# Front stage of a two-layer hybrid block: x normalised token-major before the transposes, convolution and gate fed straight from PSUM

## The chip, the cores and the metric

One core of a Trainium2 chip runs the kernel. The metric is the device time of one execution in microseconds (us), here as the median of three runs. TensorE (PE) multiplies, VectorE (DVE) and ScalarE (ACT) work element by element, GpSimd (POOL) does small side work, and SyncE's queue (SP) issues the loads and stores. TensorE writes to PSUM (banks of 128 partitions by 512 fp32 values), which VectorE and ScalarE can read; everything else lives in SBUF.

## The reference, cut to what matters

A block of two layers over 512 tokens of width 1024. The change touches the first mixer only, in layer 0:

```python
def rmsnorm(x, w):
    xf = x.astype(jnp.float32)
    xf = xf * lax.rsqrt(jnp.mean(xf * xf, axis=-1, keepdims=True) + NORM_EPS)
    return (xf * w.astype(jnp.float32)).astype(x.dtype)
...
def ssd_mixer(u, w_in, conv_w, conv_b, dt_bias, a_log, d_skip, norm_w, w_out):
    proj = u @ w_in
    z = proj[..., :SSD_D_INNER]
    xbc = jax.nn.silu(dwconv_centred(proj[..., SSD_D_INNER:SSD_D_INNER + SSD_CONV_DIM], conv_w, conv_b))
    dt_raw = proj[..., SSD_D_INNER + SSD_CONV_DIM:].astype(jnp.float32)
    ...
    y = y.reshape(bsz, seq, SSD_D_INNER) * jax.nn.silu(z.astype(jnp.float32))
...
    for i in range(DEPTH):
        u = rmsnorm(h, mix_norm_w[i])
        ...
        h = h + mix
        h = h + conv_ffn(rmsnorm(h, ffn_norm_w[i]), ...)
        h = h + per_layer_embed(h, p[i], ...)
    return rmsnorm(h, final_norm_w)
```

The convolution runs over the tokens, channel by channel, with 5 taps centred on the token. The mixer (a chunked scan in both directions) has 4 groups of 8 heads.

## The kernel before, in words

Everything is kept transposed: channels on the partitions, the 512 tokens along the free dimension. `h[:, m, :]` (m = 0..7) is the residual. Each projection is computed in fp32 quality from three fp32r products: the weights are split into `w_hi` (ACT, line 974, `hi(u)`) and `w_lo` (DVE, line 1315, `lo(u)`), the input into `uh` and `ul`, and `product` (PE, lines 1916 to 1918) issues w_hi·uh, w_hi·ul and w_lo·uh.

The work of PE is cut into *units*: one load of up to 128x1024 weights, which feeds 24 matmuls of 128x512. A *pair* is two units (the two halves of the contraction) that fill two PSUM tiles. Units are numbered in one sequence (`Plan.unit`), and `w_raw`, `w_hi`, `w_lo` have two buffers each: `hi(u)` waits until unit u-2 has been multiplied, `lo(u)` waits for `hi(u)`, the load of u waits for `lo(u-2)`. `hi_to` and `lo_to` issue them at fixed places of ACT's and DVE's programs.

All projections go through `ring`, four PSUM banks in rotation: tile t is written into bank t % 4, and PE waits on the semaphore `evac` until tile t-4 has been taken out. `evac` counts the tiles in their order. The other PSUM banks are `pe_e` (2), `pe_y` and `pe_s`.

**Start.** SP loads x (one 2 MB DMA), then 19 small DMAs of parameters into `stage` and `step_in`, 3 more small ones, then the weights. PE waits for all 19, transposes the seven parameter tiles, then x, tile by tile, into `ring`. For each of the 8 tiles DVE copies it to `h`, ACT squares it and makes `uh`, DVE makes `ul`, POOL adds up the squares; PE sums them over the partitions with a ones matrix (`pe_s`), DVE and ACT turn that into `rstd`, the same row of 512 values on every partition (`rstd_of(0)`). Unit 0 is the `dt` projection (64 columns). `uh` and `ul` carry x times the norm's weight but not `rstd`: every projection of this layer is multiplied by `rstd` as it is taken out of PSUM.

**Each group g** has 3 pairs `xbc` (x in two pairs, B and C in the third), 2 pairs `z` and, from g = 1, the four `out` units of the group before. For an `xbc` pair DVE multiplies both tiles by `rstd` into `cin` (line 1430, this frees the banks), ACT does the first tap (line 1056), DVE the other four on each tile (line 1440, 8 instructions), ACT the silu (line 1065). For a `z` pair DVE multiplies by `rstd` into `zs` (`take_z`, line 1452) and ACT applies silu in place. After the third pair come transposes of x and B, the products with the masks, the states and their decays, and for each of 4 head pairs the decay rows (ACT, lines 1087 and 1097), their weighting (DVE, 1486 to 1488) and the output products (PE, 2059); at the end of the group DVE and ACT normalise y (lines 1592 to 1604), while PE works on the first units of the next group.

After the four groups come two feed-forward blocks, the gates and the second mixer. The change does not touch their arithmetic.

## Time and profile before

| | |
|---|---|
| time, median of 3 runs | 1782.2 us (1780.02 to 1782.22) |
| span of the profiled execution | 1782.5 us |
| busy in it | PE 87%, weight loads 70%, DVE 71%, ACT 44%, POOL 13% |
| first matmul of unit 0 (`dt`) / of the first `xbc` unit | 47.29 / 56.51 us |
| first `xbc` pair taken out of PSUM from | 69.35 us |
| first `z` pair of group 0 taken from | 102.00 us |
| end of group 0, 1, 2 (line 1592) | 190.91, 320.55, 449.98 us |

The profiled execution has no other time beside its span, and the span lies 0.3 us above the median, inside the spread of the runs. Times in the rows below count from the first instruction. The table is read as a sequence: the start until 56.51 us, then group 0, then three groups of about 130 us each, then 1200 us of other work.

### The profile page before, as it was taken

How to read it: one execution, taken by the hardware profiler on the slowest of the kernel's cores; microseconds unless marked ns; L12 is line 12 of the kernel's file. 1: busy time of each engine (PE TensorE's matmuls, PEld its weight loads, DVE VectorE, ACT ScalarE, POOL GpSimd, SP SyncE). 2: the span in 40 equal slices, each digit the busy share in tenths (PEclk: the TensorE clock that was granted, in tenths of full speed). 3: DMA queues.
4: the chain of work that ended last, by engine and by line, in shares of the span. 5: the costliest groups of instructions: out<-in, count | busy, mean ns of one | idle time of the engine just before them, and what ended most of it. 6: DMA issues, size and time to landing. Idle time of an engine off the chain costs nothing.

```text
span 1782.5 us, 20153 instructions
## 1 busy us (share of the span) xinstructions
PE 1551.1 (87%) x7275; PEld 1248.1 (70%) x7275; DVE 1257.2 (71%) x1479; ACT 784.4 (44%) x1339; POOL 225.0 (13%) x224
## 2 busy tenths in 40 slices
PE   3875886987986889999998776889999999999996
PEld 1663765755754668878886564879787888888875
DVE  4577767767866788887888687897467666664355
ACT  3348456456465445522444424231235555543242
POOL 1144000000000480002007311000010000001000
PEclk7897998998998899999998988795999999999998
DMA  2223313313312343353343565693322333233231
GB/s 73 83 67 128 100 63 115 92 54 118 95 48 71 77 101 95 117 183 124 120 156 131 189 219 189 186 277 84 92 97 83 100 100 94 94 100 101 89 95 65
DMA packets 192169, 198.99 MB, mean 112 GB/s; under 512 B 47822, under 2 KB 178462, under 8 KB 187998
## 3 DMA queue, kind: packets, MB, share of 16 engines
q1 hardware_dynamic: 192094, 198.01, 35.9%
q8 instruction: 45, 0.74, 0.2%
q14 instruction: 30, 0.25, 0.0%
HBM read 169.47 MB, written 28.51 MB: 111 GB/s over the span
## 4 chain that ended last, share of the span: by engine, by line
PE 66%; DVE 15%; ACT 9%; DMA 5%; issue 3%; SPq 1%; DVEq 0%; ACTq 0%
PE ring L1916 19%; PE ring L1917 19%; PE ring L1918 19%; ACT rows L1087 3%; DVE w_lo L1315 3%; ACT rows L1097 3%; PE pe_s L2161 2%; PE ring L2145 2%; DMA w_raw<-in_ple_w_gate 2%; DMA rows<-log_decays 1%; ACT w_hi L974 1%; PE pe_s L2155 1%; PE pe_y L2059 1%; DVE cc L1440 1%; DVE cc L1806 1%
## 5 line engine op out<-in xcount | busy, mean ns | idle before, releaser
L974 ACT ACTIVATE w_hi<-w_raw 128x1024 fp32r<-128x1024 f32 (+1 forms) x233 | 239.6, 1028 | 621.7 <-PE ring L1918 572.4
L1916 PE MATMUL ring<-uh,w_hi 128*128 128x512 f32 (+1 forms) x1160 | 462.0, 398 | 41.4 <-DVE w_lo L1315 30.0
L1917 PE MATMUL ring<-ul,w_hi 128*128 128x512 f32 (+1 forms) x1160 | 455.6, 393 | 0.0
L1918 PE MATMUL ring<-uh,w_lo 128*128 128x512 f32 (+1 forms) x1160 | 454.9, 392 | 0.0
L1315 DVE TENSOR_TENSOR w_lo<-w_raw,w_hi 128x1024 fp32r<-128x1024 f32 (+1 forms) x233 | 281.7, 1211 | 180.2 <-ACT w_hi L974 179.9
L1916 PEld LDWEIGHTS ring<-uh,w_hi 128*128 128x128 f32 (+1 forms) x1160 | 219.8, 190 | 99.5 <-DVE w_lo L1315 27.5
L1918 PEld LDWEIGHTS ring<-uh,w_lo 128*128 128x128 f32 (+1 forms) x1160 | 219.7, 189 | 47.5 <-issue 0.6
L1917 PEld LDWEIGHTS ring<-ul,w_hi 128*128 128x128 f32 (+1 forms) x1160 | 220.0, 190 | 47.1 <-issue 2.1
L1916 PE MATMUL ring<-gh,w_hi 128*128 128x512 f32 x480 | 189.5, 395 | 19.3 <-DVE w_lo L1315 17.6
L1918 PE MATMUL ring<-gh,w_lo 128*128 128x512 f32 x480 | 188.0, 392 | 0.0
L1917 PE MATMUL ring<-gl,w_hi 128*128 128x512 f32 x480 | 188.0, 392 | 0.0
L1806 DVE SCALAR_TENSOR_TENSOR cc<-cin,par,cc 128x512 f32<-128x512 f32 x176 | 128.3, 790 | 1.0 <-ACT cc L1251 1.0
L1916 PEld LDWEIGHTS ring<-gh,w_hi 128*128 128x128 f32 x480 | 91.0, 190 | 41.7 <-DVE w_lo L1315 18.9
L1795 DVE TENSOR_TENSOR cin<-ring,rstd 128x512 f32<-128x512 f32 x88 | 56.7, 686 | 77.3 <-PE ring L1918 77.3
L1918 PEld LDWEIGHTS ring<-gh,w_lo 128*128 128x128 f32 x480 | 90.8, 189 | 19.4
L1917 PEld LDWEIGHTS ring<-gl,w_hi 128*128 128x128 f32 x480 | 91.1, 190 | 18.5
L1087 ACT ACTIVATE rows<-rows,ad_seq 128x128 f32<-128x128 f32 x256 | 76.4, 386 | 19.0 <-DMA rows<-log_decays 19.0
L2059 PE MATMUL pe_y<-rows,xseq 128*64 128x128 f32 x256 | 38.3, 372 | 52.3 <-DVE xT L1500 50.1
L1097 ACT ACTIVATE rows<-rows,dt_seq 128x128 f32<-128x128 f32 x256 | 76.4, 386 | 0.0
L1251 ACT ACTIVATE cc<-cin,par 128x512 f32<-128x512 f32 x88 | 66.7, 806 | 16.1 <-DVE cin L1795 16.1
L2059 PEld LDWEIGHTS pe_y<-rows,xseq 128*64 128x64 f32 x256 | 32.8, 191 | 56.5 <-DVE xT L1500 53.0
L753 POOL TENSOR_TENSOR var<-sq 128x512 f32<-128x512 f32 x7 | 10.0, 1425 | 484.1 <-ACT sq L990 423.0
(280 smaller groups left out, 2157.8 us busy)
## 6 DMA issues: line engine op xcount, KB each, us to landing
w_raw<-in_ffn_w_up SPq DMA_DIRECT2D x88, 512.0 KB, 3.5
w_raw<-in_ffn_w_down SPq DMA_DIRECT2D x40, 512.0 KB, 3.5
w_raw<-in_ssd_w_in SPq DMA_DIRECT2D x32, 512.0 KB, 4.0
rows<-log_decays SPq DMA_DIRECT2D x16, 1024.0 KB, 6.0
s_tables<-tab SPq DMA_DIRECT2D x16, 1024.0 KB, 5.3
slot<-s_tables SPq DMA_DIRECT2D x16, 1024.0 KB, 7.4
w_raw<-in_ssd_w_out SPq DMA_DIRECT2D x16, 512.0 KB, 3.5
w_raw<-in_ple_w_gate SPq DMA_DIRECT2D x16, 512.0 KB, 3.5
```

Source lines behind the costliest of these rows:

```text
L974: act.activation(w_hi[u % 2][:, 0:n], w_raw[:, u % 2, 0:n], ACT.Copy).then_inc(hi_done, 1)
L1087: act.activation(row, row, ACT.Relu, scale=-1.0, bias=cs_seq[:, c, at:at + 1]).then_inc(fall_done, 1)
L1097: act.activation(row, row, ACT.Exp, scale=-1.0, bias=dt_ln[:, c, at:at + 1]).then_inc(exp_done, 1)
L1251: act.activation(cc[:, 2 * half + j, :], cin[:, j, 1:1 + SEQ], ACT.Identity, scale=dcol(i * 2 + (C_FCW + c)), bias=dcol(i * 2 + (C_FCB + 2 ...
L1315: dve.tensor_tensor(w_lo[u % 2][:, 0:n], w_raw[:, u % 2, 0:n], w_hi[u % 2][:, 0:n].bitcast(F32), ALU.subtract).then_inc(lo_done, 1)
L1795: dve.tensor_tensor(cin[:, j, 2:2 + SEQ], bank(t + 2 * half + j), rstd[:], ALU.mult).then_inc(evac, 1)
L1806: dve.scalar_tensor_tensor(out=cc[:, 2 * half + j, :], in0=cin[:, j, 1 + tap:1 + tap + SEQ], scalar=dcol(i * 2 + (C_FCW + c)), in1=cc[:, 2 ...
L1916: pe.matmul(o, wh[:, k, c], rh[:, k0 + k, :], start=first and k == 0, stop=False)
L1917: pe.matmul(o, wh[:, k, c], rl[:, k0 + k, :], start=False, stop=False)
L1918: mm_ = pe.matmul(o, wl[:, k, c], rh[:, k0 + k, :], start=False, stop=last and k == nk - 1)
L2059: mm_ = pe.matmul(pe_y[64 * k:64 * k + 64, c * P:(c + 1) * P], xseq[:, c, (2 * hp + k) * HD:(2 * hp + k + 1) * HD], rows_[n % 3][:, 0, k, ...
L2145: mm_ = pe.matmul(ring[:, 2 * (b % 2) + a, NCH * g:NCH * g + NCH], slots[b % 4][:, 0, at:at + P], ul[:, b % 3, g, :], start=True, stop=True)
```

## The change

Part one, the start. x is loaded in four DMAs of 128 tokens, ahead of 9 parameter DMAs; the other 10 and the 3 small ones go behind the first two loads of weights. While tokens are still on the partitions, DVE squares and sums each piece (`tensor_tensor_reduce`), one tiny chain gives 1/rms of every token, and DVE scales x by it into `xn`. PE transposes `xn` into `ring`; ACT makes `uh` and DVE `ul` directly from PSUM, so `uh`/`ul` now hold the normalised input and no later projection needs `rstd`. The raw x, which the residual `h` needs, is transposed apart: half of it at once into the four PSUM banks that are free then (`spare`), half after the first pair, with the remaining parameter tiles; ACT copies these out. The `dt` unit moves behind the third `xbc` pair.

Part two, in every group. The centre tap (shift 0) is done by ACT from PSUM, and the other four taps by DVE from PSUM, on the part of the row where they fall inside the sequence; `evac` now counts at the last tap of a tile. `z` is read by ACT's silu straight from PSUM. `cin` and `take_z` with their 24 and 16 multiplications fall away.

Some semaphores of the second layer are shared where before there was one each; SP now waits for three saves (`t_late`) where it waited for two.

```diff
-        tile("params", 2)
+        tile("params", 1)
         tile("x", 8)
-        tile("dt", 1, True)
         for g in range(groups):
             tile(("xbc", g), 6, True)
+            if g == 0:
+                tile("dt", 1, True)
...
-            sp.dma_start(x_in[:], A["x"][0].rearrange("(b p) d -> p b d", p=P)).then_inc(in_x, 16)
+            for b in range(SB):
+                sp.dma_start(x_in[:, b, :], A["x"][0, b * P:b * P + P, :]).then_inc(in_x[b], 16)
...
-                    xbc_loads(0, 0, 6)
+                    xbc_loads(0, 0, 2)
+                    late_params()
+                    xbc_loads(0, 2, 6)
+                    load(U["dt"], rows(w_in, 0, KD, XBC0 + CONV_T * P, 2 * HEADS), k=KD)
...
+            act.wait_ge(x_step, X_VAR)
+            act.activation(x_ss[:], x_ss[:], ACT.Sqrt).then_inc(x_std, 1)
             for m in range(KD):
-                squares(0, m)
-                u_hi(0, m, uh0)
-            std(0)
+                if m == 4:
+                    hi_to(1)
+                act.wait_ge(filled, FILL["x"] + m + 1)
+                if m == 0:
+                    act.wait_ge(evac, 1)
+                act.activation(uh0[:, m, :], bank(T["x"] + m), ACT.Identity, scale=col(C_MIX + m)).then_inc(x_uh, 1)
...
+            def spares(n0, n1):
+                for n in range(n0, n1):
+                    act.wait_ge(spare_full, n + 1)
+                    dst = h[:, n, :] if n < KD else (par[:, 2 * P:6 * P], par[:, 6 * P:7 * P])[n - KD]
+                    act.activation(dst, spare(n)[:, 0:dst.shape[1]], ACT.Copy).then_inc(spare_taken, 1)
+            spares(0, 4)
...
                     hi_to(u + 2 * i + 3)
                     if g == 0:
                         if i == 0:
+                            spares(4, KD + 2)
+                            act.wait_ge(spare_taken, KD + 2)
                             vec(V_STEP, par[:, C_STEP:C_STEP + S5G], ACT.Exp)
...
-                        act.wait_ge(evac, T[("xbc", g)] + 2 * i + j + 1)
+                        act.wait_ge(unit_done, u + 2 * i + 2)
...
-                        act.activation(cc[:, q % 4, :], cin[:, q % 2, 0:SEQ], ACT.Identity,
-                                       scale=col(C_CONVW + chans[j]), bias=col(C_CONVB + chans[j])).then_inc(tap0, 1)
+                        act.activation(cc[:, q % 4, :], bank(T[("xbc", g)] + 2 * i + j), ACT.Identity,
+                                       scale=col(C_CONVW + 2 * CONV_T + chans[j]), bias=col(C_CONVB + chans[j])
+                                       ).then_inc(tap0, 1)
...
+                    act.wait_ge(unit_done, z + 2 * i + 2)
+                    if g:
+                        act.wait_ge(yl_done, GT * g)
+                    act.wait_ge(evac, T[("z", g, i)])
                     for j in range(2):
-                        act.wait_ge(evac, T[("z", g, i)] + j + 1)
-                        act.activation(zs[:, 2 * i + j, :], zs[:, 2 * i + j, :], ACT.Silu).then_inc(z_silu, 1)
+                        act.activation(zs[:, 2 * i + j, :], bank(T[("z", g, i)] + j), ACT.Silu).then_inc(evac, 1)
...
+            for b in range(SB):
+                dve.wait_ge(in_x[b], 16)
+                dve.tensor_tensor_reduce(out=xn[:, b, :], in0=x_in[:, b, :], in1=x_in[:, b, :], scale=1.0, scalar=0.0,
+                                         op0=ALU.mult, op1=ALU.add, accum_out=x_ss[:, b:b + 1]).then_inc(x_step, 1)
...
-                    for j in range(2):
-                        dve.tensor_tensor(cin[:, j, 2:2 + SEQ], bank(T[("xbc", g)] + 2 * i + j), rstd[:], ALU.mult
-                                          ).then_inc(evac, 1)
                     lo_to(u + 2 * i + 3)
-                    for tap in range(1, 5):
+                    for n, shift in enumerate(SHIFTS):
...
+                            op = dve.scalar_tensor_tensor(
+                                out=cc[:, q % 4, a:b], in0=bank(T[("xbc", g)] + 2 * i + j)[:, a + shift:b + shift],
+                                scalar=col(C_CONVW + (2 + shift) * CONV_T + chans[j]), in1=cc[:, q % 4, a:b],
+                                op0=ALU.mult, op1=ALU.add)
+                            op.then_inc(*((taps, 1) if n < 3 else (evac, 1)))
```

VectorE at the start of the program, before the change, up to the first `lo`. The names in it are the tiles above; x8 is a count of equal neighbours.

```order
L1353 COPY stage<-step_in 64x128
L1345 COPY par<-ring 128x512
L1357 COPY par<-ring 128x384
L1345 COPY h<-ring 128x512
L1329 SCALAR_TENSOR_TENSOR ul<-h,par,uh 128x512
L1345 COPY h<-ring 128x512
L1329 SCALAR_TENSOR_TENSOR ul<-h,par,uh 128x512
```

VectorE at the same place after the change; the ISA rows are the sums of squares and the reading of their sums (four of each).

```order
L1391 ISA xn,x_ss<-x_in 128x1024
L1391 ISA x_ss 128x1
L1394 TENSOR_SCALAR x_ss<-x_ss 128x4
L1382 COPY par<-ring 128x256
L1397 RECIPROCAL x_rs<-x_ss 128x4
L1400 TENSOR_SCALAR xn<-x_in,x_rs 128x1024 x4
L1407 SCALAR_TENSOR_TENSOR ul<-ring,par,uh 128x512 x4
L1352 TENSOR_TENSOR w_lo<-w_raw,w_hi 128x1024
L1407 SCALAR_TENSOR_TENSOR ul<-ring,par,uh 128x512 x4
```

The eight copies to `h` have left VectorE, the squares are sums over whole rows, and the first `lo` stands after the fourth `ul`.

VectorE where group 0 ends and group 1 begins, before the change: the normalisation of y, then the first pair's convolution.

```order
L1315 TENSOR_TENSOR w_lo<-w_raw,w_hi 128x1024
L1600 SCALAR_TENSOR_TENSOR zs<-xT,par,ytmp 128x512 x4
L1604 TENSOR_TENSOR yl<-zs,yh 128x512 x4
L1430 TENSOR_TENSOR cin<-ring,rstd 128x512 x2
L1315 TENSOR_TENSOR w_lo<-w_raw,w_hi 128x1024
L1440 SCALAR_TENSOR_TENSOR cc<-cin,par,cc 128x512 x8
L1315 TENSOR_TENSOR w_lo<-w_raw,w_hi 128x1024
L1430 TENSOR_TENSOR cin<-ring,rstd 128x512 x2
```

The same place after the change.

```order
L1352 TENSOR_TENSOR w_lo<-w_raw,w_hi 128x1024
L1632 SCALAR_TENSOR_TENSOR zs<-xT,par,ytmp 128x512 x4
L1636 TENSOR_TENSOR yl<-zs,yh 128x512 x4
L1352 TENSOR_TENSOR w_lo<-w_raw,w_hi 128x1024
L1481 SCALAR_TENSOR_TENSOR cc<-ring,par,cc 128x510 x2
L1481 SCALAR_TENSOR_TENSOR cc<-ring,par,cc 128x511 x4
L1481 SCALAR_TENSOR_TENSOR cc<-ring,par,cc 128x510 x2
L1352 TENSOR_TENSOR w_lo<-w_raw,w_hi 128x1024 x2
```

The two `cin` rows are gone; nothing else has changed its place there.

ScalarE in group 0 between its first two rounds of `hi` and the second pair, after the change (before it, the two L1061 and L1087 rows followed the `hi` rows directly).

```order
L988 ACTIVATE w_hi<-w_raw 128x1024 x2
L1029 ACTIVATE h<-pe_e 128x512 x2
L1029 ACTIVATE h<-pe_y 128x512
L1029 ACTIVATE h<-pe_s 128x512
L1029 ACTIVATE par<-pe_e 128x512
L1029 ACTIVATE par<-pe_e 128x128
L1061 ACT_TABLE_LOAD
L1061 ACTIVATE v<-par 128x64
L1087 ACTIVATE cc<-ring,par 128x512 x2
```

Six copies out of the spare banks now stand ahead of the first pair's centre taps.

## Rows read from the trace of the kernel before

**Rows 1.** Busy time by stretch: engine busy (count), granted clock, DMA share.

```profile
core 0: us, PE busy (x) PEld busy (x) DVE busy (x) ACT busy (x) POOL busy (x), PEclk, DMA share, GB/s
0.00:47.26 47.26, 14.14 (x45) 8.27 (x46) 21.26 (x26) 14.60 (x21) 8.69 (x20) 0.71 0.21 69
47.26:54.64 7.38, 7.31 (x24) 3.88 (x24) 0.00 (x0) 0.00 (x0) 0.00 (x0) 0.76 0.23 71
54.64:56.51 1.87, 0.00 (x0) 0.00 (x1) 1.87 (x3) 1.06 (x1) 0.00 (x0) 1.00 0.00 0
56.51:69.35 12.84, 12.84 (x49) 10.44 (x50) 2.31 (x2) 1.06 (x1) 0.00 (x0) 0.87 0.41 122
69.35:101.97 32.62, 32.62 (x146) 26.96 (x145) 27.55 (x36) 20.36 (x26) 15.08 (x25) 1.00 0.31 83
...
190.90:320.55 129.65, 107.86 (x473) 81.44 (x472) 94.40 (x122) 71.26 (x170) 2.53 (x2) 0.93 0.29 90
```

**Rows 2.** Timeline of the start: start, length, engine, line, what; idle before it.

```profile
0.81 0.45 SPq L451 DMA_DIRECT2D x_in<-in_x  x1
10.36 0.60 SPq L475 DMA_DIRECT2D step_in<-in_s_log_step  x1
14.66 3.32 PE L1944 MATMUL ring<-eye,x_in 128*128 128x128 f32 x20
20.52 1.12 PE L1944 MATMUL ring<-eye,x_in 128*128 128x128 f32 x4 [2.55 <-DVE h L1345]
24.93 1.25 DVE L1329 SCALAR_TENSOR_TENSOR ul<-h,par,uh 128x512 fp32r<-128x512 f32 x1 [1.31 <-ACT uh L994]
```

**Rows 3.** DMA issues of the start: count, size, median us from issue to landing.

```profile
x_in<-in_x SPq DMA_DIRECT2D x1, 2048.0 KB, 8.0
w_raw<-in_ssd_w_in SPq DMA_DIRECT2D x4, 512.0 KB, 5.2
```

**Rows 4.** Stretches behind the pause at 54.64 us, columns as in Rows 1.

```profile
59.00:61.00 2.00, 2.00 (x6) 1.52 (x6) 0.00 (x0) 0.00 (x0) 0.00 (x0) 0.50 0.99 321
61.00:63.00 2.00, 2.00 (x10) 1.65 (x9) 0.00 (x0) 0.00 (x0) 0.00 (x0) 1.00 0.18 61
```

**Rows 5.** Groups by form, 0 to 620 us: count, busy, mean ns, idle before.

```profile
L1493 DVE SCALAR_TENSOR_TENSOR xT<-xT,d_col,pe_e 128x512 f32<-128x512 f32 x16 | 11.8, 740 | 0.0
L1600 DVE SCALAR_TENSOR_TENSOR zs<-xT,par,ytmp 128x512 f32<-128x512 f32 x16 | 10.9, 745 | 0.0
L1392 DVE TENSOR_SCALAR rows<-rows,hvec 64x512 f32<-64x512 f32 x1 | 0.5, 478 | 0.0
L1022 ACT ACTIVATE rows<-pe_e 64x512 f32<-64x512 f32 x1 | 0.6, 590 | 5.1 <-PE pe_e L1969 5.1
L1031 ACT ACT_TABLE_LOAD x2 | 2.6, 1283 | 0.0
```

**Rows 6.** Timeline at the start of group 1, VectorE and then TensorE.

```profile
201.88 1.28 DVE L1430 TENSOR_TENSOR cin<-ring,rstd 128x512 f32<-128x512 f32 x2
203.08 1.21 DVE L1315 TENSOR_TENSOR w_lo<-w_raw,w_hi 128x1024 fp32r<-128x1024 f32 x1
204.22 5.38 DVE L1440 SCALAR_TENSOR_TENSOR cc<-cin,par,cc 128x512 f32<-128x512 f32 x8
209.52 1.21 DVE L1315 TENSOR_TENSOR w_lo<-w_raw,w_hi 128x1024 fp32r<-128x1024 f32 x1
...
204.35 0.50 PE L1916 MATMUL ring<-uh,w_hi 128*128 128x512 f32 x1 [1.65 <-DVE w_lo L1315]
...
210.79 0.50 PE L1916 MATMUL ring<-uh,w_hi 128*128 128x512 f32 x1 [0.70 <-DVE w_lo L1315]
```

**Rows 7.** Timeline behind the second z pair of group 1, VectorE, then ScalarE.

```profile
249.04 1.29 DVE L1452 TENSOR_TENSOR zs<-ring,rstd 128x512 f32<-128x512 f32 x2 [8.34 <-PE ring L1918]
250.25 2.35 DVE L1315 TENSOR_TENSOR w_lo<-w_raw,w_hi 128x1024 fp32r<-128x1024 f32 x2
252.51 0.68 DVE L1345 COPY car<-ring 128x512 f32<-128x512 f32 x1
...
263.36 1.06 ACT L974 ACTIVATE w_hi<-w_raw 128x1024 fp32r<-128x1024 f32 x1 [1.38 <-PE ring L1918]
```

More of the change, by code:

```diff
@@ L74, in __init__ @@
         units = 0
-        mixer = [("dt", 1)]
+        mixer = []
         for g in range(groups):
-            mixer += [(("xbc", g), 6), (("z", g), 4)] + ([(("out", g - 1), 4)] if g else [])
+            mixer += [(("xbc", g), 6)] + ([("dt", 1)] if g == 0 else [])
+            mixer += [(("z", g), 4)] + ([(("out", g - 1), 4)] if g else [])
         mixer += [(("out", groups - 1), 4)]
@@ L170, in bidir_hybrid_kernel @@
         step_in = sb("step_in", [S5G, 2], where=start)
+        x_ss = sb("x_ss", [P, SB], where=start)
+        x_rs = sb("x_rs", [P, SB], where=start)
+        xn = sb("xn", [P, SB, D], where=start)
         start.close()
@@ L423, in unit_size, with saved_u @@
             return 1024
+        def saved_u(b):
+            return (u_saved[b % 3], 16 * (b // 3) + 16) if b < 6 else (u_saved[b - 3], 16)
         def loads_by(u):
@@ L601, in s5_loads @@
                     sp.wait_ge(tab_saved[i], 16 * NB)
-                for n in range(NB):
+                for n in range(5):
                     sp.wait_ge(t_saved[n], 16)
@@ L1063, in _ @@
                         dst = xT[:, 2 * i + j, :] if i < 2 else (bT, cT)[j][:]
-                        act.wait_ge(taps, 8 * (3 * g + i) + 6 + j + 1)
+                        act.wait_ge(evac, T[("xbc", g)] + 2 * i + j + 1)
                         act.activation(dst, cc[:, q % 4, :], ACT.Silu).then_inc(silu, 1)
+                if g == 0:
+                    dt_take()
                 hi_to(z + 3)
@@ L1425, in _ @@
                     chans = [g * GT + 2 * i, g * GT + 2 * i + 1] if i < 2 else [INNER // P + g, INNER // P + GROUPS + g]
[L1426 to L1431 removed]
                     lo_to(u + 2 * i + 3)
[L1433 removed]
+                    for n, shift in enumerate(SHIFTS):
                         for j in range(2):
                             q = 6 * g + 2 * i + j
[L1436 removed]
+                            if n == 0:
                                 dve.wait_ge(tap0, q + 1)
                             else:
[L1439 to L1453 removed]
+                                dve.wait_ge(taps, 6 * pr + 2 * (n - 1) + j + 1)
+                            a, b = max(0, -shift), SEQ - max(0, shift)
+                            op = dve.scalar_tensor_tensor(
[3 more added lines that the diff above has]
+                            op.then_inc(*((taps, 1) if n < 3 else (evac, 1)))
+                    lo_to(u + 2 * i + 4)
                 def take_out(g, i):
@@ L1538, in _ @@
                 if g:
-                    take_z(1)
                     lo_to(z + 5)
+                    dve.wait_ge(evac, T[("state", g, 0)])
                 for n in range(6):
@@ L1995, in _ @@
                     for kg in range(2):
+                        if g == 0 and i == 0:
+                            pe.wait_ge(evac, T["x"] + 4 * kg + 4)
                         product(u + 2 * i + kg, T[("xbc", g)] + 2 * i, 4, 4 * kg, uh0, ul0, first=kg == 0, last=kg == 1)
+                        if g == 0 and (i, kg) == (0, 1):
+                            late_transposes()
                         if g and (i, kg) == (0, 0):
                             group_square(g - 1, GT - 1)
+                if g == 0:
+                    product(U["dt"], T["dt"], KD, 0, uh0, ul0, tiles=1, width=2 * HEADS)
                 z_product(0)
```

217 lines of the change are left out of this document (110 added, 107 removed).

## The prediction, written before the changed kernel ran

> **What bounds the kernel now.** I read the busy times by stretch first [rows 1]. Before 56.51 us PE is busy for 21.5 us, and in two thirds of that with things that are not projections: the start is a chain, not a throughput problem. From 69.35 to 101.97 us PE is full: three pairs, 144 matmuls of 512 columns in 32.62 us, so 0.2265 us each, 5.44 us a unit and 10.87 us a pair. In a later group PE works 107.9 of 129.65 us and DVE 94.4, so each group has stretches in which something else ends the wait. To find which, I read the timeline.
>
> At the start [rows 2, 3] x lands 8.0 us after its issue, at 8.8 us, but PE stands still until the last of 19 parameter DMAs, issued at 10.36 us, has been spread; then the x tiles crawl because a tile passes PE, DVE, ACT and DVE in turn, and `ul` takes 1.25 us. At the start of group 1 [rows 6] PE waits for DVE: `yl` ends at 201.88, then come `cin` (1.20 us to the next row), `lo`, eight taps (5.30 us), `lo`, and only then, at 210.79, PE starts the fifth unit of the group (0.70 us idle on the row, and 1.65 us at the unit before). From there PE runs without a gap to the z pair. Behind the second z pair [rows 7] PE and ACT wait for DVE again: 1.21 us of `zs`, two `lo` in 2.26 us, then the first state copy at 252.51; everything down to ACT's `hi` at 263.36, which waits for PE, hangs on it.
>
> **The start, step by step.** The first xbc pair comes out at 69.35 us now. After the change:
>
> - x has landed at 8.8 us as before, since the four DMAs move the same 2 MB ahead of all else. The last piece's sum of squares: no row shows this instruction. Bounds: 1.21 us (two SBUF inputs, 1024 long, the `lo` of [rows 6]) and twice that. I take 1.2, it has the same inputs: 10.0.
> - Three tiny operations over DVE and ACT and the copy of two parameter tiles; 0.2 us each and 0.4 us by estimate from the lengths in [rows 5]: 11.1. ACT's table for the square root is loaded ahead, while it waits.
> - Four scalings of 128x1024: one SBUF input and a column scalar took 0.478 us for 512 [rows 5]. Bounds 0.75 and 1.21 each. I take 0.75, the same form: 14.1.
> - First four tiles. PE's transposes run at 0.166 us each at the full clock and about 0.23 at the lower [rows 2], so 0.66 to 0.93 a tile. With the lower one, 17.8; then `uh` 0.7 (an estimate: a bit over the 0.59 of ACT's row in [rows 5]), `hi` 1.05, `lo` 1.2 [rows 6, 7]: unit 0 starts near 20.8. The first weights land 5.2 us after an issue at about 7 [rows 3], so they wait, not PE. The other four tiles need about 4.5 us on ACT and DVE and are hidden behind unit 0.
> - Units 0 and 1: 10.9 us, plus a start at the lower clock. In this trace the granted clock was 0.50 in a stretch behind a pause of 1.87 us [rows 1, 4], and the first pair took 12.84 us in place of 10.88 (its two units less the boundary). I add 1.9.
>
> The pair ends at 33.6 us: 35.7 us earlier.
>
> **What is given back in group 0.** Behind the first pair PE has work that it had done before: 21 transposes (3.6 us at 0.166; 4.8 at 0.23), and the `dt` unit, 24 matmuls of 512 columns, now in the middle of a full PE: 5.4 us. The transposes ask for little, so I expect the clock to drop once more behind them as at 54.64 to 56.51: 1.6 us. ACT stands longer: after `hi` six copies (0.55 to 0.59 each [rows 5], together with `hi` 4.3 us), a table load and the exponential (1.5), then the taps. With 0 at the end of the first pair: centre taps 5.8 to 7.3, DVE's eight taps 6.6 to 12.0 and `lo` to 13.2. PE is at 14.5 by then (3.6 of transposes and a pair), so ACT's queue is covered by 1.3 us; if the cover went, the price would be that excess. The third pair is finished at 25.4, `dt` at 30.8. Its taps are the ones that count: two of the four banks are held until the last tap, and z's first unit must wait for one of them. `hi` of the unit ahead to 26.5, two small sines, centre tap, then taps from 27.7, the first tile's last at 32.5: 1.7 us of waiting. Sum given back: 3.6 + 5.4 + 1.6 + 1.7 = 12.3. Net gain before the end of z's first pair: 35.7 - 12.3 = 23.4 us. The rest of group 0 runs as before: there z's silu waits for a table load (1.28), which takes the place of the two multiplications.
>
> **What each later group gains.** At its start `cin` goes, 1.2 us of DVE in a chain that PE waits for [rows 6]. The centre tap on ACT no longer waits for `cin`, and is ready before `lo` ends. The banks: PE's fifth unit writes where the first pair stood, and now needs its last tap, at 203.0 + 5.3 = 208.3; the `lo` behind it ends at 209.5 anyway, so the hold costs nothing, by 1.2 us of cover. For the next two pairs DVE needs 5.3 + 2.3 us in PE's 10.9, and ACT's `hi`, silu, `hi`, centre tap about 4; taps start near 7 and 2 us after the pair, and end 3 us before their bank is asked for. Behind the second z pair `take_z` goes and one `lo` moves ahead of the wait: the copy that stood 3.47 us behind the pair stands behind `hi` and `lo`, 1.06 + 1.2: 1.2 us. ACT's two silus there stay where they were, behind one `hi`, so the decays behind them start no later, and at 263.36 ACT had been idle for 1.38 us, so it lets the gain through. Sum 2.4 us for each of groups 1, 2, 3: 7.2 us. What a tap costs from PSUM is the one price this rests on. In [rows 5] the same instruction with a PSUM input took 740 ns, without one 745: no difference.
>
> The Trainium skill gives VectorE a longer fixed time for PSUM sources, 120 cycles against 58 (VectorE: DVE Perf Modes, the section on the TRN2 errata). That speaks against this change: by it the eight taps are an estimated 0.5 us longer, the gain of three groups is 5.7 us, and the total is 1753. By the rows there is nothing to subtract; they decide.
>
> In the second layer SP waits for a third save, a few us of an interval in which it is ahead; I count nothing. Sum: 23.4 + 7.2 = 30.6 us off 1782.5, which has the median's place within 0.3: **1751.6**.
>
> **Rivals.**
>
> *The groups give nothing* (0.15): the hold of banks, or ACT's reordered queue, eats the 2.4 us. For it: PE's cover at the fifth unit is 1.2 us. Against: DVE's chain is shorter by whole instructions. Time 1782.5 - 23.4 = 1759.
>
> *The sums of squares run at half rate* (0.12): each of the four takes 2.4 us. Pieces land some 1.5 us apart, so the last one ends near 13.4 in place of 10.0, and the whole start moves by 3.4: 1755. For it: an instruction that adds up beside two SBUF inputs has no row. Against: none either. The Trainium skill says that this family with two non-bf16 SBUF sources halves its throughput (Vector Engine (DVE) Microarchitecture Reference, Points that are easy to get wrong); no trace here shows it.
>
> *The clock stays up and the banks are free in time* (0.10): 1.9 + 1.6 + 1.7 us fewer, 1746. For it: after the first 51 us PE has few pauses. Against: the row of 0.50 came after one below 2 us.
>
> *Slower: taps from PSUM run as `ul` did beside POOL, 1.25 us each* (0.03). Then each pair needs 8 x 1.25 + 2.3 us of DVE, more than PE's 10.9, and with ACT's 3.5 us in series a pair of banks comes free 2.6 us late, 12 times (31 us), and the chain into the fifth unit is 4.7 us longer, 4 times (19 us): 1752 + 50 = 1802. It decides from about 1.05 us a tap. Against it: the 740 ns row, taken while PE ran.
>
> *The start doesn't shorten* (0.01): the four pieces of x would have to land as late as everything together did. Against: 8.0 us for 2 MB. Time 1775 to 1785.
>
> **How the numbers follow.** Forecast as worked out: 0.59. Low end: the clock rival and one more us in each group, 1743. High end: half-rate squares together with the scalings at 1.21 (1.9 us), or no group gain with a little of either: 1762. Beyond that lie some of the mixed cases and the slower one. Faster by over 0.2% (3.6 us, about what a measurement of this kernel can tell from no change): 0.96; the same 0.01; slower 0.03.
>
> **What would show each step.** The first xbc matmul near 21 us, and the end of the first pair near 34; an idle PE of 1 to 2 us ahead of z in group 0 that ends with a tap; z's first pair of group 0 finished near 78.5. The fifth unit of group 1 starts 7.7 us after `yl` ends (8.9 now); the first state copy 2.3 us behind z's second pair; group lengths (from one line-1624 instruction to the next) of 127.2 us. Taps of 0.74 us. Wrong it would be if taps take over 1 us, if PE waits for banks between xbc pairs, or if x lands in pieces later than 9 us.

## The result, and the profile after

The changed kernel takes 1754.6 us (median of 4 runs, 1748.3 to 1756.3) against 1782.2 us before: ratio 0.983, 95% interval 0.981 to 0.986. The forecast was 1751.6 us, range 1743 to 1762, faster at 0.96. Sign and time came out as predicted, the time with some luck: single terms of the start were off by 1.0 to 1.6 us both ways and partly cancelled, the groups gave less than their 7.2 us in this trace, and runs of one kernel differ by as much as single terms (the next four runs of the changed kernel had a median of 1749.0 us).

The profiled execution took 1753.23 us with a span of 1751.4 us, 31.1 us less than the 1782.5 us before; between the medians of the runs it is 27.6 us. The windows by stretch (core 0; us, then busy time of each engine with its count, granted clock, DMA share, GB/s) answer to [rows 1]:

```profile
0.00:22.29 22.29, 12.48 (x51) 9.43 (x51) 15.88 (x27) 8.31 (x12) 2.40 (x15) 1.00 0.51 162
22.29:34.89 12.60, 12.60 (x48) 10.16 (x49) 3.65 (x5) 3.15 (x6) 0.00 (x0) 0.86 0.38 114
34.89:37.58 2.69, 2.65 (x23) 2.44 (x22) 1.23 (x1) 2.43 (x5) 0.00 (x0) 1.00 0.09 27
37.58:77.70 40.12, 38.48 (x170) 30.13 (x170) 22.52 (x30) 21.49 (x31) 8.79 (x25) 1.00 0.31 84
166.55:295.67 129.12, 110.00 (x473) 82.78 (x472) 88.35 (x111) 70.88 (x170) 2.53 (x2) 0.93 0.28 90
295.67:422.55 126.88, 107.94 (x473) 81.36 (x472) 88.35 (x111) 70.83 (x170) 2.53 (x2) 0.93 0.29 92
```

The first `xbc` pair ends at 34.9 us, not 69.35. Behind it stand 2.7 us of transposes at the full clock. A later group has 88.4 us of DVE in place of 94.4, the 6 us of the removed multiplications, but lasts 129.1 or 126.9 us, in place of 129.65.

The timeline of the start (start, length, engine, line, what, idle time before it and its releaser), against [rows 2]:

```profile
4.57 1.23 DVE L1391 CUSTOM_DVE_ANT_0 xn<-x_in 128x1024 f32<-128x1024 f32 x1 [1.59 <-DMA x_in<-in_x]
8.50 1.23 DVE L1391 CUSTOM_DVE_ANT_0 xn<-x_in 128x1024 f32<-128x1024 f32 x1
...
11.13 0.42 DVE L1382 COPY par<-ring 128x256 f32<-128x256 f32 x1 [1.19 <-PE ring L1973]
11.68 2.74 DVE L1400 TENSOR_SCALAR xn<-x_in,x_rs 128x1024 f32<-128x1024 f32 x4
...
15.79 3.23 DVE L1407 SCALAR_TENSOR_TENSOR ul<-ring,par,uh 128x512 fp32r<-128x512 f32 x4 [1.37 <-ACT uh L1022]
19.20 1.23 DVE L1352 TENSOR_TENSOR w_lo<-w_raw,w_hi 128x1024 fp32r<-128x1024 f32 x1 [0.19 <-ACT w_hi L988]
20.73 2.73 DVE L1407 SCALAR_TENSOR_TENSOR ul<-ring,par,uh 128x512 fp32r<-128x512 f32 x4 [0.30 <-ACT uh L1022]
22.29 0.47 PE L1948 MATMUL ring<-uh,w_hi 128*128 128x512 f32 x1 [1.89 <-DVE ul L1407]
```

The sum of squares of a piece (the custom instruction) takes 1.23 us for 1024 columns, so the half-rate rival is out. The last line is the surprise of the start: `lo` of unit 0 is done at 20.4 us (the forecast had 20.8), and PE still waits for `ul`, its first product starting at 22.29 behind 1.89 us of idleness.

TensorE's one wait in group 0 ahead of z, then VectorE and TensorE at the start of group 1 against [rows 6], and VectorE's state copy behind the second z pair against [rows 7]:

```profile
66.55 0.47 PE L1948 MATMUL ring<-uh,w_hi 128*128 128x512 f32 x1 [1.64 <-DVE cc L1481]
...
177.53 1.22 DVE L1352 TENSOR_TENSOR w_lo<-w_raw,w_hi 128x1024 fp32r<-128x1024 f32 x1
178.67 5.34 DVE L1481 SCALAR_TENSOR_TENSOR cc<-ring,par,cc 128x510 f32<-128x510 f32 x8
183.92 1.21 DVE L1352 TENSOR_TENSOR w_lo<-w_raw,w_hi 128x1024 fp32r<-128x1024 f32 x1
...
178.80 0.50 PE L1948 MATMUL ring<-uh,w_hi 128*128 128x512 f32 x1 [0.44 <-DVE w_lo L1352]
185.19 0.50 PE L1948 MATMUL ring<-uh,w_hi 128*128 128x512 f32 x1 [0.61 <-DVE w_lo L1352]
...
225.65 0.68 DVE L1382 COPY car<-ring 128x512 f32<-128x512 f32 x1
```

`yl` ends at 177.53 and the fifth unit starts at 185.19: 7.7 us, the forecast to the tenth (8.9 before). Eight taps from PSUM take 5.34 us, from SBUF they took 5.38 (with 510 or 511 columns each now, 512 then).

### The profile page after: what moved, and what is told of

It is laid out like the page before. It is cut to its first block, busy times and chain, and to the rows that moved or that the text cites. A ratio compares the mean times of both kernels' runs of the same rounds, so it can differ in the third digit from the quotient of the medians.

```text
span 1751.4 us, 20143 instructions
## 1 busy us (share of the span) xinstructions
PE 1551.1 (89%) x7301; PEld 1248.7 (71%) x7301; DVE 1227.2 (70%) x1441; ACT 780.9 (45%) x1340; POOL 213.7 (12%) x219
## 4 chain that ended last, share of the span: by engine, by line
PE 69%; DVE 13%; ACT 9%; DMA 5%; issue 3%; SPq 0%; DVEq 0%; ACTq 0%
PE ring L1948 20%; PE ring L1949 20%; PE ring L1950 20%; ACT rows L1124 3%; ACT rows L1134 2%; PE pe_s L2216 2%; DVE w_lo L1352 2%; PE ring L2200 2%; DMA w_raw<-in_ple_w_gate 2%; ACT w_hi L988 1%; DMA rows<-log_decays 1%; DVE cc L1481 1%; PE pe_y L2114 1%; PE pe_s L2210 1%; DVE ytmp L1626 1%
## 5 line engine op out<-in xcount | busy, mean ns | idle before, releaser
L1948 PE MATMUL ring<-uh,w_hi 128*128 128x512 f32 x1160 | 461.3, 398 | 32.6 <-DVE w_lo L1352 23.2
L1949 PE MATMUL ring<-ul,w_hi 128*128 128x512 f32 x1160 | 455.0, 392 | 0.0
L1950 PE MATMUL ring<-uh,w_lo 128*128 128x512 f32 x1160 | 454.1, 391 | 0.0
L1948 PEld LDWEIGHTS ring<-uh,w_hi 128*128 128x128 f32 x1160 | 219.4, 189 | 88.6 <-DVE w_lo L1352 21.3
L1950 PEld LDWEIGHTS ring<-uh,w_lo 128*128 128x128 f32 x1160 | 219.4, 189 | 47.3
L1949 PEld LDWEIGHTS ring<-ul,w_hi 128*128 128x128 f32 x1160 | 219.6, 189 | 46.9 <-issue 1.7
L1288 ACT ACTIVATE cc<-cin,par 128x512 f32<-128x512 f32 x88 | 66.7, 805 | 12.7 <-DVE cin L1827 12.7
L1481 DVE SCALAR_TENSOR_TENSOR cc<-ring,par,cc 128x510 f32<-128x510 f32 (+1 forms) x96 | 64.1, 739 | 4.6 <-ACT cc L1087 4.6
```

The lines of the kernel that those rows point to most:

```text
L1288: act.activation(cc[:, 2 * half + j, :], cin[:, j, 1:1 + SEQ], ACT.Identity, scale=dcol(i * 2 + (C_FCW + c)), bias=dcol(i * 2 + (C_FCB + 2 ...
L1481: op = dve.scalar_tensor_tensor(out=cc[:, q % 4, a:b], in0=bank(T[("xbc", g)] + 2 * i + j)[:, a + shift:b + shift], scalar=col(C_CONVW + ( ...
L1948: pe.matmul(o, wh[:, k, c], rh[:, k0 + k, :], start=first and k == 0, stop=False)
L1949: pe.matmul(o, wh[:, k, c], rl[:, k0 + k, :], start=False, stop=False)
L1950: mm_ = pe.matmul(o, wl[:, k, c], rh[:, k0 + k, :], start=False, stop=last and k == nk - 1)
```

## Where the 31.1 us are

I follow marks that both traces have: VectorE's first `xseq` copy (the end of group 0's projections), the first addition of an output tile to `h` in each group (h0), the second (h1), and the group's end (the `var` instruction). All times in us, each a start from the timelines:

| mark | before | after | after, second trace (E1) |
|---|---|---|---|
| first product | 47.29 | 22.29 | 22.10 |
| first `xseq` copy | 104.34 | 80.02 | 78.26 |
| end of group 0 | 190.91 | 166.55 | 166.01 |
| end of group 3 | 575.47 | 546.43 | 544.56 |
| span | 1782.5 | 1751.4 | 1745.9 |

In the first trace 24.3 us are gained before group 0's `xseq`, 4.7 in groups 1 to 3, and 2.1 in the 1200 us behind group 3, where the change does nothing (1207.0 against 1205.0; 1201.3 in the second trace). So the start has its predicted 23.4 and 0.9 more, the groups have 4.7 of the predicted 7.2, and 2.1 are not the change's. That left two questions: what the groups' missing 2.5 us are, and which step of the start was misjudged.

## The experiments

**E1, the changed kernel again** (a_again). No edit.

> The changed kernel once more, for a second trace of it. In the first trace group 1 kept 24.9 us of the 27.0 us that it was ahead at the first output tile, because the granted clock was 0.82 to 0.87 in two stretches of 5 us near 230 and 250 us; group 2 had no such loss behind its output tile. If those stretches belong to the program, they stand at the same places again and the group ends lie within 0.2 us of 166.6, 295.7, 422.6 and 546.4. If the clock's drops depend on where a chip happens to be in its own rhythm, the work between them has the same durations, but group 1, 2 or 3 differ by 1 to 2 us from the first trace, and the total lies anywhere from 1748 to 1757.

1749.0 us (1747.6 to 1754.9, 4 runs). The group lengths changed places: 126.9, 129.1, 122.6, where the first trace had 129.1, 126.9, 123.9. In detail, h0 minus the end of the group before (A), h1 minus h0 (B), end of group minus h1 (C), groups 1, 2, 3:

| | A | B | C |
|---|---|---|---|
| before | 72.39, 72.39, 70.82 | 16.85, 16.85, 18.52 | 40.40, 40.19, 36.15 |
| after | 69.78, 69.94, 69.78 | 18.45, 16.84, 18.43 | 40.89, 40.10, 35.67 |
| after, E1 | 70.00, 69.83, 69.96 | 16.85, 18.47, 16.87 | 40.05, 40.75, 35.77 |

B has two values, 16.85 and 18.45, for the same instructions. The windows of group 1 around the same idle stretch (2.52 us in the first trace, 2.53 in the second) show why, the changed kernel's first trace first, then E1's:

```profile
223.33:226.99 3.66, 1.71 (x5) 0.40 (x4) 2.48 (x4) 3.57 (x9) 0.00 (x0) 1.00 0.03 7
226.99:231.33 4.34, 4.33 (x7) 2.13 (x8) 4.27 (x8) 4.32 (x12) 0.00 (x0) 0.61 0.36 115
240.33:247.01 6.68, 3.76 (x9) 1.15 (x8) 6.44 (x11) 6.68 (x25) 0.00 (x0) 1.00 0.00 0
247.01:252.33 5.32, 5.32 (x19) 4.28 (x20) 4.09 (x4) 5.32 (x20) 0.00 (x0) 0.68 0.01 3
```

```profile
223.01:226.68 3.67, 1.72 (x5) 0.55 (x4) 2.65 (x4) 3.67 (x10) 0.00 (x0) 1.00 0.07 20
226.68:231.22 4.54, 4.47 (x9) 2.28 (x10) 4.47 (x8) 4.51 (x13) 0.00 (x0) 0.65 0.29 99
240.01:246.69 6.68, 3.77 (x8) 1.15 (x7) 6.44 (x11) 6.68 (x25) 0.00 (x0) 1.00 0.00 0
246.69:252.01 5.32, 5.31 (x26) 4.47 (x27) 4.10 (x4) 5.32 (x20) 0.00 (x0) 1.00 0.01 3
```

Same work, same 6.68 us with 3.8 us of PE, but then 5.3 us with a mean clock of 0.68 in one and 1.00 in the other, and 1.6 us between them at h1. At the end of the group it is 2.2 us (129.12 against 126.90), since C differs too. The fall behind the states, in A, stood in all six groups of the two traces; the one in B comes and goes, as the theory of a rhythm has it, and the total fell in its 1748 to 1757. What decides it is not shown.

The start varies in the same way. In E1 the first `xbc` pair ran at the full clock:

```profile
22.10:33.12 11.02, 11.02 (x49) 9.05 (x50) 3.66 (x5) 3.15 (x6) 0.00 (x0) 1.00 0.44 130
```

It took 11.02 us there and 12.60 in the first trace, at a mean clock of 0.86.

**E2 and E3, the copies put back in groups 1 to 3** (b1, b2). E2 copies the convolution's banks to `cin` first (edit below, with the waits that belong to it); E3 also puts DVE's copies of the z banks back.

```diff
+                    if g:
+                        dve.wait_ge(unit_done, u + 2 * i + 2)
+                        dve.wait_ge(taps, t0)
+                        for j in range(2):
+                            dve.tensor_copy(cin[:, j, 2:2 + SEQ], bank(T[("xbc", g)] + 2 * i + j)).then_inc(evac, 1)
```

> As the changed kernel, but in groups 1 to 3 DVE first copies each convolution bank to SBUF and the taps read the copy. My theory (the copy stood on the path into the fifth unit of a group): the fifth unit starts 8.7 us after yl ends, in place of 7.5, and the first output tile of groups 1 to 3 comes 1.2 us later each time; total 3.6 us over the changed kernel, 1757. Rival, that the hold of banks costs as much as the copy: total unchanged at 1753, and PE waits before the z pair now in the changed kernel. Rival, that taps are dearer from PSUM: eight taps here take less than 5.30 us.

> As b1, and in groups 1 to 3 DVE copies the gate's banks before silu too, so that only the start and group 0 of the change are left. Theory: start and group 0 alone are worth 24 us and the groups 2.4 us each where no clock drop eats it; total 1760, 7 us over the changed kernel, the first state copy of group 1 stands 3.5 us behind the z pair, and the first output tile of group 1 is 24.4 us earlier than before the change, against 27.0 in the changed kernel. Rival, the clock gives the groups' gain back anyway: total 1755 to 1756, with group lengths within 0.5 us of the changed kernel's in sum.

E2: 1755.7 us (1753.2 to 1760.6), E3: 1759.9 us (1758.6 to 1760.3). E2's timeline at the start of group 1, VectorE then TensorE:

```profile
178.72 1.28 DVE L1479 COPY cin<-ring 128x512 f32<-128x512 f32 x2
179.92 1.22 DVE L1354 TENSOR_TENSOR w_lo<-w_raw,w_hi 128x1024 fp32r<-128x1024 f32 x1
181.05 5.39 DVE L1491 SCALAR_TENSOR_TENSOR cc<-cin,par,cc 128x512 f32<-128x512 f32 x8
...
181.19 0.50 PE L1964 MATMUL ring<-uh,w_hi 128*128 128x512 f32 x1 [1.63 <-DVE w_lo L1354]
187.63 0.50 PE L1964 MATMUL ring<-uh,w_hi 128*128 128x512 f32 x1 [0.70 <-DVE w_lo L1354]
```

The fifth unit starts 8.9 us behind `yl` (ending 178.72), and A is 70.97, 70.89, 70.91: 1.1 us more than the changed kernel, three times. That is the convolution's term (1.2 predicted). Both rivals of E2 fall by these marks; its total, 1.1 us over the changed kernel's first four runs and 6.7 over the next four, can't tell. In E3 the first state copy stands 61.6 us behind the end of group 0 (227.50 - 165.88), 1.2 more than E2's 60.4 (228.17 - 167.75), which is the gate's term; but its A is 73.41, 70.79, 70.79. The windows around the states of E3 in groups 1, 2 and 3 say what happened (TensorE only):

```profile
228.00:236.00 8.00, 7.16 (x15) 0.57 0.36 122
355.00:364.00 9.00, 5.79 (x19) 1.00 0.36 117
484.00:493.00 9.00, 5.79 (x18) 1.00 0.40 119
```

In groups 2 and 3 the clock did not fall there. The same holds for group 3 of the kernel before (70.82, clock 1.00 from 511 to 519 us) and for group 1 of E8 (68.33, clock 1.00 from 222 to 231 us). So A must be compared like for like: with a fall 72.39 against 69.8, without one 70.82 against 68.33. Both say 2.5 to 2.6 us at h0 for the two passes that the change took away, where the forecast had 2.4. (Group 1 of E3, 73.41, had the clock at a mean of 0.57 over 8 us and compares with none.) The lengths of whole groups with a fall in A and none in B say about the same: 129.64 and 129.43 us before, 126.88 and 126.90 after, 2.7 us less. The total of E3 came out at the theory's 1760; over the changed kernel's first median it is 5.3 us, and the lengths of its three groups are 4.9 us longer in sum, where the rival had them within 0.5.

**E4, x in one load.**

```diff
-            for b in range(SB):
-                sp.dma_start(x_in[:, b, :], A["x"][0, b * P:b * P + P, :]).then_inc(in_x[b], 16)
+            sp.dma_start(x_in[:], A["x"][0].rearrange("(b p) d -> p b d", p=P)).then_inc(in_x[0], 16)
```

> x comes in one DMA of 2 MB in place of four pieces, all else as in the changed kernel. Theory: the pieces let three of four sums of squares run under the load; with one load they start near 8.8 us and end at 13.9 in place of 9.7, PE's first product moves by 4.1 us, from 22.3 to 26.4, and the total is 1757. Rival, the first product waits for something else (weights, parameters, a bank): it moves by less than 2 us.

1760.0 us (1751.9 to 1767.5). E4's timeline:

```profile
8.74 1.23 DVE L1390 CUSTOM_DVE_ANT_0 xn<-x_in 128x1024 f32<-128x1024 f32 x1 [5.76 <-DMA x_in<-in_x]
...
13.53 0.42 DVE L1381 COPY par<-ring 128x256 f32<-128x256 f32 x1
14.11 2.74 DVE L1399 TENSOR_SCALAR xn<-x_in,x_rs 128x1024 f32<-128x1024 f32 x4
...
24.73 0.47 PE L1947 MATMUL ring<-uh,w_hi 128*128 128x512 f32 x1 [2.56 <-DVE ul L1406]
```

The sums end 3.7 us later (13.41 against 9.73), but the parameter copy no longer waits for PE, which costs 1.19 us in the changed kernel, and the first product moves by 2.4 us only. Loading in pieces is worth 2.4 us here because something else is next in line: neither the theory's 4.1 nor the rival's under 2. At the first `xseq` copy it is 2.6 us (80.86 against E1's 78.26, neither with a fall at the start). The total moved by more, within a wide spread (below).

**E5, E6 and E7, dearer taps** (taps_090, taps_130, taps_125). A write that nothing reads behind each tap, to test the price of the slower rival.

```diff
                             op.then_inc(*((taps, 1) if n < 3 else (evac, 1)))
+                            if 8 * pr + 2 * n + j:
+                                dve.wait_ge(padded, 8 * pr + 2 * n + j)
+                            dve.memset(cin[:, 0, 2:2 + 512], 0.0).then_inc(padded, 1)
```

> As the changed kernel, with a write of 128 columns (which nothing reads) behind every tap on DVE, so that a tap costs some 0.9 us in place of 0.67. My working puts the point from which banks are late at 1.05 us a tap: below it only the chain into the fifth unit grows, by 8 x 0.23 = 1.8 us in each of four groups, total 1753 + 7 = 1760, and PE has no new wait between convolution pairs. Rival, there is no cover and every tap's cost counts: 96 x 0.23 = 22 us, 1775.

> As taps_090, with a write of 512 columns, so that a tap costs some 1.3 us, as in the prediction's slower rival. That rival's price: banks come free late in every pair and the chain into the fifth unit is some 5 us longer; 1802, a little more at 1.3 than at 1.25 (1808), slower than the kernel before the change. If PE's own work still covers the hold between pairs, only the chain counts: 4 x 5 = 20 us, 1773, and PE waits for taps only ahead of the fifth unit.

> As taps_130 with a longer write behind each tap. That kernel's tap came every 1.09 us, not 1.3; this one should come near 1.25 us, the price of the prediction's slower rival. By its working: chain into the fifth unit 4 x 4.6 us, and banks late by 2.6 us, 12 times: 1754 + 50 = 1804. What the trace of the 1.09 us kernel suggests instead: PE waited for the chain into the fifth unit alone (4.10 us against 0.61) and for no bank between the pairs behind it, so 4 x 4.6 us plus what DVE's own 8 x 1.25 + 2.3 = 12.3 us a pair exceed PE's 10.9, 1.4 us for the second and third pair of each group: 1754 + 18 + 11 = 1783.

The three kernels' taps came every 0.69, 1.09 and 1.30 us, not 0.9, 1.3 and 1.25: a write of 128 columns added 0.03 us to the tap's period of 0.66, where I had reckoned with 0.23. So the first (1757.2 us, 2 runs) tests nothing; its A of 69.95 to 70.24 is the changed kernel's. At 1.09 us the time is 1775.4 us (1768.4 to 1782.6), near the 1773 of the reading in which only the chain into the fifth unit counts; at 1.30 us it is 1792.4 us (1786.0 to 1794.2), slower than before the change (ratio 1.005, 1.002 to 1.007). TensorE in group 1 of the last:

```profile
201.59 0.79 PE L1954 MATMUL ring<-uh,w_hi 128*128 128x512 f32 x1 [5.85 <-DVE w_lo L1353]
214.78 0.50 PE L1954 MATMUL ring<-uh,w_hi 128*128 128x512 f32 x1 [0.24 <-DVE w_lo L1353]
227.45 1.09 PE L2067 MATMUL ring<-eye,xT 128*128 128x128 f32 x8 [1.49 <-ACT cT L1098]
```

PE waits for the chain into the fifth unit (5.85 us, 0.61 in the changed kernel) and hardly for a bank: in groups 1 to 3 `cc` releases none of its waits of this stretch; in group 0 it does, 4.86 us at 74.81. The rival's 50 us at 1.25 had too much in the banks; at a still dearer 1.30 it is 38. The second working of E7's expectation, redone afterwards for 1.30 (4 x 5.0 us of chain, 8 pairs with 12.7 us of DVE in PE's 10.9), gives 1754.6 + 20 + 14 = 1789. Between the two measurements a straight line crosses 1782.2 at 1.17 us a tap.

**E8 and E9, the start reordered** (weights_early, weights_params). E8 puts ACT's `hi_to(0)` and DVE's `lo_to(0)` ahead of the x tiles (edit below), E9 also moves DVE's copy of the first parameters behind the first scaling.

```diff
             act.activation(x_ss[:], x_ss[:], ACT.Sqrt).then_inc(x_std, 1)
+            hi_to(0)
             for m in range(KD):
-                if m == 4:
+                if m == 6:
                     hi_to(1)
...
             dve.wait_ge(evac, 1)
+            lo_to(0)
             for m in range(KD):
-                if m == 4:
-                    lo_to(0)
```

> As the changed kernel, but ACT rounds the first weights and DVE takes the rest of them before the x tiles, where both wait for PE. In the changed kernel the first product started at 22.29 us, when the sixth x tile was taken: its output bank is that tile's. Theory: the 1.23 us that DVE spent on the weights between the fourth and fifth tile were on that path, and it starts at 20.9; the first pair ends 1.4 us earlier, total 1.4 us less (1752). Rival, the product waits for the weights' landing: the x tiles are late instead and the product starts at 22.3 or later.

> As weights_early, and DVE copies the first two parameter tiles behind the first scaling of x instead of ahead of the reciprocal, where it had waited 1.19 us for PE. Theory: the scalings end 0.9 us earlier and so does the first product: 20.0 us, total 2.3 us below the changed kernel (1751). Rival, PE's transposes for the parameters are late and hold the x tiles in any case: no difference to weights_early.

E8's timeline:

```profile
14.03 1.22 DVE L1353 TENSOR_TENSOR w_lo<-w_raw,w_hi 128x1024 fp32r<-128x1024 f32 x1
15.40 5.02 DVE L1407 SCALAR_TENSOR_TENSOR ul<-ring,par,uh 128x512 fp32r<-128x512 f32 x6 [0.15 <-ACT uh L1023]
...
20.57 0.47 PE L1948 MATMUL ring<-uh,w_hi 128*128 128x512 f32 x1 [0.70 <-DVE ul L1407]
```

The first product starts at 20.57 us, 1.5 to 1.7 us earlier, when the sixth `ul` is done: the wait at 22.29 was one for the output bank, and the theory holds.

E8 also shows what a fall behind the states is worth. Its group 1 had none, and its group 2 had one: A is 68.33 and 69.92, but B is 18.02 and 16.87, and the groups last 126.88 and 126.84 us. In group 1 VectorE, asked earlier, waits for ScalarE behind the first additions:

```profile
235.41 1.23 DVE L1353 TENSOR_TENSOR w_lo<-w_raw,w_hi 128x1024 fp32r<-128x1024 f32 x1 [1.08 <-ACT w_hi L988]
```

So 1.2 of the 1.6 us at h0 are given back at h1, and in this trace the rest by the end of the group.

E9 starts at 20.05, 0.5 us earlier and not 0.9 (its last piece of x also came 0.4 us later). The first `xseq` copy starts at 76.69 and 76.19 us against 78.26 in E1, which like them had no fall at the start: 1.6 and 2.1 us, where 1.4 and 2.3 were expected. Group 0 ends at 164.7 and 164.0 us against 166.6 and 166.0. The totals, 1749.8 (1745.0 to 1755.9) and 1750.8 (1749.6 to 1753.0), can't be told from the changed kernel's 1754.6 and 1749.0.

**E10, more of the start's work ahead of the tiles** (all_early). E9, and the 16 transposes of the second half of raw x ahead of the first tile, ACT's copies of the first half before them.

```diff
+            spares(0, 4)
             hi_to(0)
...
+            for n in range(4, KD):
+                pe.wait_ge(spare_taken, n - 3)
+                for b in range(SB):
+                    mm_ = pe.transpose(spare(n)[:, b * P:(b + 1) * P], x_in[:, b, n * P:(n + 1) * P], eye[:])
+                mm_.then_inc(spare_full, 1)
```

> As weights_params, and the 16 transposes of the other half of raw x move from behind the first pair (where PE was full) to ahead of the first x tile, with ACT's copies of the first half ahead of them. Theory: the part behind the first pair shrinks from 2.6 us to 0.8 us, the first product stays near 20 us, group 0 ends 1.8 us before that of weights_params (162.2 against 164.0), total 1.8 us less, 1749. Rival, the transposes hold up the x tiles: PE had only some 2 us free there, so the first product is 1 to 2 us later and nothing is won.

1748.9 us (1740.4 to 1753.2). Group 0 ends at 162.3 us, as the theory said (162.2); the first product is at 20.41, 0.4 us later than E9's, a little of what the rival expected. From the first product to the first `xseq` copy it is 54.16 us in place of 56.14: moving PE work from a full stretch to an idle one was worth 2.0 us, less the 0.4.

**E11 and E12, PE kept busy in idle stretches** (pe_filled, all_filled). E11 is the changed kernel with products into a free bank; E12 adds them to E10.

```diff
+                def warm(n):
+                    for k in range(n):
+                        pe.matmul(pe_s[:], uh0[:, k % KD, 0:P], uh0[:, k % KD, :], start=k == 0, stop=k == n - 1)
...
+                    if n == 2 and g:
+                        warm(8)
                     pe.wait_ge(xd_done, 6 * g + n + 1)
...
+                if g:
+                    warm(10)
                 transposes(0)
```

> As the changed kernel, but in groups 1 to 3 PE multiplies into a free bank while it would stand idle: 8 products of 512 columns (1.8 us) ahead of the third state, where it was idle 1.95 us, and 10 (2.3 us) ahead of the transposes of yo, where it was idle 2.52 us. Nothing reads the result. Two traces of the changed kernel had group lengths of 129.1/126.9/123.9 and 126.9/129.1/122.6, with the granted clock at 0.5 for some 3 us behind each idle stretch of 1.95 us and behind some of those of 2.52 us. Theory (the drops come from those idle stretches): behind both places the clock stays at 1.0, a group with two drops loses them, and the groups take about 125.3/125.3/121; total 3 to 8 us below the changed kernel, 1746 to 1751. Rival, the clock drops for other reasons (load, heat, a rhythm of its own): drops of the same length appear elsewhere in the group, and the lengths stay at 127 and 129; total 1754. Rival, the filling delays what it stands ahead of: lengths over 129.

> all_early and pe_filled together, with a third filling of 6 products ahead of the third product with the carried state, where pe_filled left PE idle for 1.58 us, and 7 in place of 10 ahead of the transposes of yo, since the ten ended 0.6 us too late. Theory (idle stretches of PE bring the half clock, which costs a group up to 2.1 us): the clock stays at 1.0 from the second z pair to the second output pair in all of groups 1 to 3, no group takes more than 127 us, and the total is 2 us below all_early's 1748.9: 1747, with a narrower spread than its 1740 to 1753. Rival, the drops move to another idle stretch again, as in group 1 of pe_filled: a group of 128.5 us or more stays, total 1749.

E11: 1750.5 us (1745.7 to 1759.5). The windows of its group 1 and 2:

```profile
223.00:238.00 15.00, 14.43 (x48) 8.46 (x46) 10.12 (x15) 14.97 (x43) 0.00 (x0) 1.00 0.10 36
238.00:246.00 8.00, 6.43 (x13) 2.90 (x13) 7.62 (x13) 8.00 (x29) 0.00 (x0) 0.79 0.00 0
351.00:365.00 14.00, 13.83 (x47) 8.53 (x47) 8.70 (x13) 13.65 (x38) 0.00 (x0) 1.00 0.13 39
365.00:381.00 16.00, 13.83 (x53) 8.74 (x51) 13.43 (x18) 16.00 (x56) 0.00 (x0) 1.00 0.01 2
```

The fall behind the states is gone in all groups (A 68.33, 68.28, 68.34), but in group 1 one came behind another idle stretch, of 1.57 us ending at 239.2 us, and B was 19.30, 18.03, 18.02 although the last two have the clock at 1.00. The 18.0 is the 1.08 us for which DVE, asked earlier, waits for ACT's `hi`, as in group 1 of E8, which has no fillings; the fillings delay only group 1, where the ten end 1.4 us after `yo` is ready. Lengths: 128.6, 126.8, 122.2.

E12: 1746.2 us (1744.8 to 1753.9, 5 runs), the lowest median of all, 0.981 of before (0.979 to 0.983). The windows around states and first head pair in its three groups (222 to 252, 349 to 379 and 476 to 506 us) have a clock of 1.00, and the groups take 126.4, 126.3 and 122.1 us, where the changed kernel took 126.9, 126.9 and 122.6 with a fall in A alone: the theory's bound of 127 holds, and no fall has moved to a group's other stretches at their cost. The fillings are worth 0.5 us a group against a fall in A, and more where B had one. Group 3 ends at 537.0 us, 9.4 us before the changed kernel's first trace. The median is 8.3 us below the changed kernel's first four runs and 2.7 below its second four, with overlapping intervals, so that it beats the changed kernel is likely but not shown by the times. The spread of its five runs, 9.1 us, is below the 12.7 of E10's four and above the 8.0 and 7.3 of the changed kernel's: too few runs to say that it narrowed.

**Why totals scatter.** The unchanged part behind group 3 took from 1201.1 (E8) to 1214.3 us (E11 and E12) in 14 traces with the same instructions. What differs with it is the clock in the second mixer; the windows from 1090 to 1240 us of E8 and then E12 (TensorE only):

```profile
1090.00:1240.00 150.00, 136.23 (x1023) 0.86 0.62 174
```

```profile
1090.00:1240.00 150.00, 138.52 (x905) 0.74 0.59 164
```

That is why E12's profiled execution took 1753.0 us in spite of its early group 3, and why I read differences of a few us from marks and not from totals.

## Why the prediction was right, step by step

- **Landing and sums of squares:** last sum done at 9.73 us, predicted 10.0; 1.23 us each. The Trainium skill's rule of half throughput (Vector Engine (DVE) Microarchitecture Reference, Points that are easy to get wrong) is not what this instruction shows, if it is of the form that the rule names, which no trace says: 1024 columns with two SBUF sources took what `lo` takes.
- **Tiny operations and parameters:** 11.68 for 11.1. The term missed DVE's 1.19 us for PE's parameter transposes. The scalings were right, 2.74 us for 4 x 0.75 less overlap, end 14.4 for 14.1.
- **Start of unit 0:** predicted 20.8, measured 22.3. This step failed: "the other four tiles ... are hidden behind unit 0". They are hidden from the data but not from the banks; unit 0 writes where x tiles 4 and 5 stand, and waits until both are taken. E8 removed 1.5 to 1.7 us by taking `lo` out of their way.
- **Units 0 and 1:** 12.6 us for 12.8. The clock did fall at the start, predicted from the 12.84 us of [rows 1], but that was luck of one trace: in E1 it did not, and the pair took 11.0. The pair ends at 34.9 for 33.6 (33.1 in E1).
- **Given back in group 0:** late transposes 2.6 for 3.6 us, z's bank 1.64 for 1.7. The 1.6 us for a fall of the clock behind the transposes were wrong: PE had no idle time there, and the clock stayed at 1.00 from 34.89 to 77.70 us. This and the 1.0 too much for the transposes, 2.6 us in sum, more than made up for the 1.3 too little before. First z pair finished at 77.7 us, 78.5 predicted.
- **Groups:** 2.4 us each predicted, 2.5 to 2.7 measured like for like, but 4.7 in sum in the first trace and 6.0 in the second, not 7.2. The step that failed is not in the terms but in adding them to one trace of before: that trace had two falls of the clock in A and one in B, the changed kernel's had three and two. Of the groups' missing 2.5 us the added fall in B, in group 1, is 2.2 (its length against E1's). Group 3, with the added fall in A, gained 1.6 us; how much more it would have gained without that fall no run shows.
- **Taps from PSUM:** 5.34 to 5.36 us for eight, 5.38 before. The Trainium skill's longer fixed time (VectorE: DVE Perf Modes, the section on the TRN2 errata) would have made it an estimated 0.5 us more; the traces don't agree: E2, with the same taps from SBUF, took 5.39.
- **The rivals:** the groups gave less for a reason that the first rival did not name. Of the clock rival (1746) two parts came true in E1, whose start and transposes ran at the full clock; z's bank was still late by 1.64 us. The half-rate rival has a slip: four sums of 2.4 us from a first piece landed at 8.8 - 4.5 = 4.3 us end at 13.9, not 13.4, and its time would be 1755.5. The slower rival's 1.05 us a tap is where DVE's work on a pair reaches PE's 10.9 us; at 1.09 PE waited for no bank between pairs, and the time of the kernel before is reached only at about 1.17.

Not settled: what decides whether an idle stretch of 1.9 to 2.5 us is followed by the half clock. Behind the states it was in six of six groups of the changed kernel's two traces, and in none of six with the stretch filled (E11, E12), so the idle stretch has a part in it. E11's fall stood behind a stretch of 1.57 us, and behind the same stretch at 238 us in E8's group 1 the clock stayed at 1.00, so its length alone does not decide.
